# A hybrid decoder step on one core: the twenty gate quarters spread over seventeen attention steps instead of fourteen

## The reference, cut to what matters

```python
h = rms_norm(x, g_mix)
a_glu, b_glu, q, k, v, qi, ki, wi, gc, ga = split(h @ w_in)        # one projection
conv_out = silu(layer_norm(depthwise_conv31(a_glu * sigmoid(b_glu)))) @ w_cout
att      = sparse_attention(rope(rms_norm(q)), rope(rms_norm(k)), v, top-k by qi, ki, wi)
x = x + (sigmoid(gc) * conv_out + sigmoid(ga) * (att @ w_aout)) @ w_o
```

## Time and profile before

| | us |
|---|---|
| median of the runs | 1489.83 |
| the profiled execution | 1490.01 |
| its span, from first to last instruction | 1488.2 |
| PE busy in the span | 1424.3 |
| DVE busy | 1050.9 |
| POOL busy | 592.2 |
| ACT busy | 548.5 |
| the steps of the loop on PE | 818.0 to 966.1 |

### The profile page before, as it was taken

The page is one execution under the profiler, slowest core; times in us unless marked ns, Lnnn a source line. Parts: engine busy times, 40 slices in busy tenths (PEclk is TensorE's granted clock), DMA queues, the critical chain, the costliest instruction groups (busy, mean ns, idle before and its releaser), DMA issues. The chain is left out here.

```text
span 1488.2 us, 20869 instructions
## 1 busy us (share of the span) xinstructions
PE 1424.3 (96%) x8219; PEld 1117.0 (75%) x8219; DVE 1050.9 (71%) x1685; ACT 548.5 (37%) x841; POOL 592.2 (40%) x414
## 2 busy tenths in 40 slices
PE   5989999999999999999999899999998999999998
PEld 2224678777888876436766566689998999999998
DVE  1356788989746899998997998567689765674221
ACT  3134655325712331122112234443374444452111
POOL 2000565444369846552345777132305455320000
PEclk9999999999999999999999999999999999999999
DMA  9995363232267878867458777332421322312222
GB/s 339 364 387 206 98 87 109 85 100 71 72 199 238 289 251 304 283 213 246 142 165 281 263 222 234 126 121 86 137 76 57 114 86 86 114 51 71 83 88 85
DMA packets 155874, 246.66 MB, mean 166 GB/s; under 512 B 11901, under 2 KB 104845, under 8 KB 155515
## 3 DMA queue, kind: packets, MB, share of 16 engines
q1 hardware_dynamic: 130734, 162.26, 33.4%
q0 software_dynamic: 23056, 76.03, 16.2%
q10 hardware_dynamic: 1989, 7.07, 1.2%
HBM read 235.48 MB, written 10.20 MB: 165 GB/s over the span
## 5 line engine op out<-in xcount | busy, mean ns | idle before, releaser
L2826 POOL TENSOR_TENSOR w_lo<-w_raw,w_hi 128x1024 fp32r<-128x1024 f32 x65 | 172.2, 2650 | 224.8 <-ACT w_hi L1352 224.6
L698 PE MATMUL ps<-bh,wqr 128*128 128x288 f32 x936 | 205.4, 295 | 4.2 <-DVE wqr L1969 1.9
L2896 POOL DMA_INDIRECT kv<-cache_v,idxT x128 | 138.0, 1078 | 96.9 <-PE ps L1130 48.8
L1352 ACT ACTIVATE w_hi<-w_raw 128x1024 fp32r<-128x1024 f32 (+1 forms) x88 | 91.3, 1037 | 225.2 <-PE ps L649 178.0
L2884 POOL DMA_INDIRECT kv<-cache_k,idxT x128 | 138.8, 1085 | 83.9 <-DVE kprod L2517 51.8
L698 PEld LDWEIGHTS ps<-bh,wqr 128*128 128x128 f32 x936 | 155.6, 188 | 5.0 <-DVE wqr L1969 3.8
L649 PE MATMUL ps<-h_hi,w_hi 128*128 128x512 f32 x352 | 138.9, 395 | 2.1 <-POOL w_lo L2826 2.1
L649 PE MATMUL ps<-h_hi,w_lo 128*128 128x512 f32 x352 | 137.3, 390 | 0.0
L649 PE MATMUL ps<-h_lo,w_hi 128*128 128x512 f32 x352 | 137.1, 390 | 0.0
L714 PE MATMUL ps<-a_hi,wqr 128*128 128x288 f32 x704 | 122.4, 295 | 0.0
L698 PE MATMUL ps<-bl,wqr 128*128 128x288 f32 x384 | 113.4, 295 | 0.0
(11 more groups left out here) (522 smaller groups left out, 3174.3 us busy)
## 6 DMA issues: line engine op xcount, KB each, us to landing
w_raw<-w_ffn_in SPq DMA_DIRECT2D x56, 512.0 KB, 3.7
wq<-w_ffn_in SPq DMA_DIRECT2D x40, 512.0 KB, 3.5
wn<-w_in SPq DMA_DIRECT2D x36, 512.0 KB, 6.2
qb<-q_scratch SPq DMA_DIRECT2D x64, 256.0 KB, 5.3
ring<-w_ffn_in SPq DMA_DIRECT2D x28, 512.0 KB, 11.1
w_raw<-w_ffn_out SPq DMA_DIRECT2D x24, 512.0 KB, 3.4
wq<-w_ffn_out SPq DMA_DIRECT2D x20, 512.0 KB, 3.4
ring<-w_ffn_out SPq DMA_DIRECT2D x14, 512.0 KB, 11.0
```

Of the source, the lines that this page charges most:

```text
L698: mm = pe.matmul(ps[:, bank + m, 0:HALF], w[:, k, m * P:(m + 1) * P], b[:, j, k, :], start=(j in (0, 1, 5) and k == 0 and fst), stop=(k == ...
L1352: act.activation(w_hi[:, slot, 0:n], w_raw[:, slot, 0:n], ACT.Copy).then_inc(S_("hi_ready"), 1)
L2826: pool.tensor_tensor(w_lo[:, slot, 0:n], w_raw[:, slot, 0:n], w_hi[:, slot, 0:n].bitcast(F32), ALU.subtract)\
L2896: pool.indirect_dma_start(kv[:, V_SLOT[j % 3] + a // 2, a % 2, :], None, rows[1], bass.IndirectOffsetOnAxis(ap=idxT[:, j % 2, t:t + 1], ax ...
```

## The change

The tuple QUARTERS gives each step its quarters. Before, steps 0, 3, 6, 9, 12 and 13 held two and the steps between them one, so that quarter 19 stood in step 13. Now steps 0, 1 and 2 hold two each and steps 3 to 16 one each, so that quarter 19 stands in step 16. The order of the quarters, their number and the steps of the sample values stay. ACT's loop reads the same tuple one step later.

```diff
-        QUARTERS = ((0, 1), (2,), (3,), (4, 5), (6,), (7,), (8, 9), (10,), (11,), (12, 13), (14,), (15,), (16, 17), (18, 19))
+        QUARTERS = ((0, 1), (2, 3), (4, 5)) + tuple((q,) for q in range(6, 20))
...
                 if 1 <= j <= 16:
                     pturn(j - 1)
-                if j < len(VALUES):
+                if j < len(QUARTERS):
                     for q in QUARTERS[j][1:]:
                         gate_quarter(q)
+                if j < len(VALUES):
                     for n in VALUES[j]:
                         values(n)
```

## The result

The changed kernel takes 1494.94 us (median of 9 runs, 1491.70 to 1498.57); the kernel before took 1491.43 us on the same chip (9 runs). The ratio is 1.0032, 95% interval 1.0018 to 1.0047: slower by 4.8 us, 2.7 to 7.0. (The ratios in this text are an estimate of their own over the runs and not the quotient of the two medians, 1.0024 here.) Repeated later, the ratio was 1.0044 (1.0027 to 1.0061), and the kernel before against itself 1.0001 (0.9988 to 1.0014). So it is slower by 0.3 to 0.4%, on the side that was forecast, and within the 0.5% that was called no change. The forecast was 1492.7.

A forecast was written before the change was run, and what follows sets the result against it. PE was taken to bound the kernel, with POOL's gathers and DVE close under it. The terms +12.0 - 8.1 - 0.5 - 1.7 + 1.2 = +2.9 us on 1489.83 gave 1492.7 us, range 1486.5 to 1498.5.

The forecast's parts named there:

- Steps 0 to 2: Loop start: the 4.35 us wait before value 15 and its slow clock go; gather 17 is issued 2.9 us later.
- POOL afterwards: Gathers after gather 17: POOL's three waits for PE, 4.45 us, go; gather 30's last issue is at 925.5.
- The waits of steps 4 to 12: PE waits about 4 us before value 18 (1.3 to 4.8); standing still for gathers makes a difference of 9.8 us.
- DVE, "under 1 us around step 8": DVE, delayed 2 us at step 3, takes 8.9 us a step to step 7 and holds PE under 1 us.
- Step 14: Step 14 begins at 939.1 instead of 947.19, -8.1 us (-9.4 to -6.3 by the landing of gather 30).
- Three late quarters, and ACT's wait: Steps 14 to 16: three quarters add 12.0 us; the 1.32 us wait for ACT in step 16 shrinks, -0.5.
- The clock at the end: Behind step 14's small products the half-clock stretch of 6.8 us becomes half as long: -1.7 us (-3.4 to +1.7).
- The tail: After the loop: quarter 19's late save makes conv_mean 1.7 to 2 us late, +1.2 us (0 to +2.4).
- The load of the merge weights: Tail: SP's load queued behind the last save's landing costs nothing, up to 1 us if it meets the gates' load.
- Rival B: POOL's gathers slow under a fuller DVE, over 5.7 us per value: +10.6 us, 1500.4 us; chance 0.08.
- Rival A: Gathers land quickly, no slow clock at the end, save lands in time: -1.3 us, 1488.5 us; chance 0.30.
- Rival C: Nothing moves: the gap's -5.9 us is balanced by equal new waits, 1489.8 us; chance 0.60 together with the forecast.

The follow-up runs named there:

- second pair: The kernel before and the changed kernel, both unchanged, run and profiled again: 1489.92 and 1494.49 us.
- first pair: The first profiles of the kernel before and the changed kernel, whose medians were 1491.43 and 1494.94 us.
- without POOL and DVE: Order of before and changed order, each with half the value gathers and 8 of 31 convolution taps left out: 1482.66 and 1487.94 us.
- the front alone: Against the kernel before, two quarters in steps 0, 1, 2, then in 9, 12 and 13, quarter 19 in step 13: 1496.22 us, 0.9986.
- the kernel with the early load: Changed kernel with the third merge unit's weights loaded ahead of the saved gates: 1503.36 us (1.0031); repeated on another chip 1492.30 us (1.0020).

## Why the prediction was right, and where its terms were off

Sign and size hold: +2.9 was forecast, 2.2 to 2.5 are in the traces up to unit 4, 3.5 lie between the medians of the first runs, and the ratios give 4.8 and 6.6. That the sum fits so well is in part luck: the terms for the waits and for the tail had the wrong cause. One by one:

- *Steps 0 to 2.* Right. No wait before value 15; gather 17's first issue was forecast 2.9 us later and is 3.1 later (846.55 - 816.18 = 30.37, against 845.29 - 818.0 = 27.29 in the earlier trace rows).
- *POOL afterwards.* Right. It waits for PE once at that issue and not again in the loop, so its 4.45 us of waits are gone. This row of its timeline is that wait, and the last issue of gather 30 is at 923.75, 1.5 earlier than before when both are counted from step 0 (forecast 1.55):

```profile
846.55 0.94 POOL L2897 DMA_INDIRECT kv<-cache_v,idxT  x1 [3.38 <-PE ps L1130]
...
923.75 0.95 POOL L2897 DMA_INDIRECT kv<-cache_v,idxT  x1 [0.30 <-issue]
```

- *The waits of steps 4 to 12.* Value 18 waited 2.26 and 2.15 us, inside the 1.3 to 4.8 but not the 4 that I took. The row for the landing was right: its product starts 5.6 us after the last issue of gather 18 (861.74 - 856.18), where I had 5.8. That issue came earlier than I had it. I had moved it by the 2.9 us of gather 17, but the eight issues from 846.55 to 856.18 took 9.6 us, and 10.9 before (845.29 to 856.20 in the earlier trace rows), so it was 1.8 us later and not 2.9. Value 30 did not wait, and what I called "PE standing still for gathers" was in part DVE.
- *DVE, "under 1 us around step 8".* This was the weak step. The wait is 0.83 us, and behind it 0.48 for ACT, so the number looks right, but it is a floor of its own and not a detail: with half of the gathers the order gains little up to step 14 (118.7, against 121.9 and 120.1), and step 9 begins at 76.6 to 76.8 in all six profiles of kernels with two quarters in each of the first three steps, a full DVE and no stop on the way. I had priced each wait beside the other, where each hides the other.
- *Step 14.* -8.1 forecast, -7.3 and, in the second pair, -10.4 measured; the kernel before has more slow clock in its gap there (6.8 us, not 3.4), and the changed one has none in the loop, where the first pair's has 3.4 twice.
- *Three late quarters, and ACT's wait.* Right: without POOL and DVE three quarters are 11.6 us, and 1.32 went to 0.74 in step 16 (-0.6).
- *The clock at the end.* -1.7 forecast. In the first pair the changed kernel has no slow stretch there and the kernel before 6.8 us; in the second each has 3.4. Its length was taken for something that the quarter decides. It is chance: the changed kernel shows 0 or 3.4, the one before 6.8 or 3.4. From step 14 to the sums an order of after takes 27.0 with 0, 28.5 to 28.7 with 3.4 and 30.2 with 6.8 us of slow clock; one of before takes 16.7, 17.4 to 17.6 and 18.6 to 19.4. So the first 3.4 us of slow clock cost 1.5 to 1.7 us there and 0.7 to 0.9 in the order of before, where PE's wait for ACT in step 16 shrinks in most of them (1.73 us without slow clock, 0.99 to 1.73 with 6.8). By these rows the clock is -2.2 us in the first pair (16.7 - 18.9) and +0.6 in the second. Over all runs of the second pair the mean granted clock is 0.9893 after and 0.9879 to 0.9886 before, 1 to 2 us in favour of the change by an estimate; but that is the clock of the whole kernel, with the gap of step 2 in it, and does not measure this term.
- *The tail, +1.2.* Right in size by luck, wrong in place. `conv_mean` waited for the save and began 6.6 us after the sums instead of 4.3 (971.60 - 965.03, 970.41 - 966.14), so 2.3 later, forecast 1.7 to 2. But unit 2 is not late: sums to unit 2 takes 15.4 to 15.5 us in every profile. PE begins the column sums of the squares at 975.50, while ACT's squares run from 973.18 to 975.88: it takes them tile by tile, and I had it wait for the last. The load of the merge weights, for which I took nothing "and up to 1 us", cost 1.8 us through ACT's queue: the square root stands behind the weights there, and I had asked only when PE needs the weights.

The sum of the first pair: -7.3 up to step 14, +8.1 from there to the sums (27.0 - 18.9), +1.8 in the tail, together +2.6, against 180.2 - 177.7 = 2.5. Of the +8.1, +10.3 is the order without slow clock (27.0 - 16.7, the latter with half the gathers and the lighter DVE) and -2.2 the clock. The quarters' +12.0 and the wait for ACT, 1.73 to 0.74 us without slow clock, make +11.0, so 0.7 us stay open.

Rival B, slower gathers under a fuller DVE, has nothing: with DVE at 56.88 of 58 us the last gather was still earlier. The rule of the Trainium skill that I set beside it (GPSIMD Engine Reference, Specifications: GpSimd shares its SBUF interfaces with VectorE) agrees with single issues, 0.94 to 1.58 us, but DVE's work was the same and the stream as a whole was not slower: from gather 17's first issue to gather 30's last it takes 77.2 us (923.75 - 846.55), and took 77.3 net of the three waits (927.03 - 845.29 - 4.45). Rival A did not hold: the save did not land in time, and its two other conditions came by chance and not together (the clock without a slow stretch in the first pair, where step 14 was 7.3 us early, and 10.4 us early in the second, against a longer slow clock in the gap of the kernel before). Rival C, which the forecast carried with it, had the loop nearly right (5.9 us of gap gone, 6.2 us of waits come), but not the end: the interval of 1.0018 to 1.0047 leaves out no change.

## What to carry to other kernels

An engine that is 100% busy may run just above several streams that are nearly as slow. Before work is moved out of a stretch, find each stream's rate there and what restarts it, because the work that leaves was cover for all of them; fill a gap with the one piece that fits it and spread the rest evenly, here every other step. And when the last of several pieces moves later, follow what waits for its landing down every queue: the cost was in a load that stood behind it and in a square root that stood behind the load.

## What was not expected of the hardware

- The clock falls to half while PE is 100% busy, behind the small products of step 14, in stretches of 3.4 or 6.8 us or not at all, in the same kernel. In the second profile of the changed kernel it also fell behind the wait of 3.00 us before unit 4. These are its windows (PE and PEld, DVE, ACT, POOL busy; granted clock, DMA share, GB/s): the wait, then the clock at about half under a full PE.

```profile
994.00:996.00 2.00, 0.02 (x1) 0.02 (x1) 2.00 (x4) 1.94 (x4) 0.00 (x0) 1.00 0.01 2
996.00:998.00 2.00, 2.00 (x8) 2.00 (x9) 1.99 (x4) 1.52 (x2) 0.40 (x1) 0.52 0.00 0
```

- 512 KB took 11.3 us to land beside 2.3 MB that took 11.6; a gather took 3.3 to 6.8 us.
- In one set of runs, whose kernel before took 1498.3 us where it took 1490 elsewhere, PE stopped for 3.36 us with no semaphore to wait for. In the profile of the front alone, the two us ahead of the product at 902.88 have a DMA share of 1.02 and no product on PE:

```profile
900.00:902.00 2.00, 0.00 (x0) 0.00 (x0) 2.00 (x6) 0.39 (x1) 1.70 (x2) 1.00 1.02 351
```

Whether PE waited there for its own instructions behind the gathers, I can't tell; no run was made for it, and the cause is open. It was not seen in the fewer gathers of the same set, nor in the other sets; the kernel with the early load had such stops in this set and none when it was repeated on another chip, so the order of the quarters alone does not make them.
